# Hybrid encoder on one core: the order of loads and of the first norms ahead of the input product

## The chip, the cores and the metric

The kernel runs on one core of a Trainium2 chip. The metric is device microseconds for one execution of the whole program; the time before is the median of three runs. The engines are PE (TensorE, matrix products), DVE (VectorE), ACT (ScalarE), POOL (GpSimd) and SP (SyncE), which here only issues DMAs. Each runs its own instructions strictly in the order of the program and meets the others at semaphores.

## What is computed

One encoder layer over a sequence of 1024 tokens and one of 512, width 1024, all float32:

```python
h = rms_norm(x, g_mix) * (1.0 + scale1) + shift1      # shift, scale: silu(c) @ w_mod + b_mod, per sequence
z = h @ w_in                                           # 1024 -> 1536
u_f, u_r, u_g = split(z, 3)
y = concat([fourier_mixer(u_f), bidirectional_rglru(conv(u_r)) * gelu(u_g)])
x = x + gate1 * (y @ w_out)
h = rms_norm(x, g_mlp) * (1.0 + scale2) + shift2
x = x + gate2 * (square(relu(h @ w_ff1)) @ w_ff2)
y = rms_norm(x, g_final)
```

The change is in the first two lines: the norm, its scaling by the conditioning map, and the first two output tiles of `h @ w_in`.

## The kernel before

Activations are kept transposed, features on the 128 partitions, tokens along the free axis. The 1536 tokens are three chunks of 512: chunks 0 and 1 are the long sequence, chunk 2 the short one. The 1024 features are eight tiles k; two tiles make a quarter q. The input product runs over 12 output tiles; the first two (j = 0, 1) are done in the front for all three chunks while the norms are still being made. Each product of float32 accuracy is three matmuls (`three`, lines 779 to 781): low part of the weights, low part of the activations, high parts. So every operand is split into hi (ACT) and lo (DVE; the later weight tiles on POOL).

The front does the following; every step has a helper of its own.

- **Norm of chunk n.** ACT squares the eight tiles (`square`, L1192), DVE adds them up (`add_squares`, seven steps, L1817), PE sums over the partitions (`norm_sum`, L796), ACT takes the root (`root`, L1197), DVE the reciprocal (`rstd`, L1732), ACT makes four diagonal blocks of it (`diagonals`, L1204), PE spreads them to all partitions (`norm_spread`, L803), ACT copies the result out (`copy_rstd`, L1251).
- **Conditioning map, quarter q.** PE multiplies `silu(c)` with a 2 MiB block of `w_mod` (`mod_quarter`, L823), ACT copies the row (`mod_copy`, L1237), PE turns it into columns (`mod_quarter_sum`, L832), DVE adds the bias and makes the amplitude (`mod_quarter_columns`, L1774 and L1778).
- **Product of chunk c, quarter q.** DVE scales x (`front_scale`, L1797), ACT adds the shift and makes hi (`front_hi`, L1245), DVE makes lo (`front_lo`, L1806), PE does 12 matmuls (`front`).
- **Weight tiles 0 and 1.** ACT makes hi (`split_win_hi`, L1217), DVE lo (`split_win_lo`, L1785).

One mod row buffer and one bank serve all four quarters, so a quarter's product waits until ACT has copied the row before it. All loads go out on SP's queue in program order: vec, chunk 0 in two halves, chunk 1, quarter 0 of `w_mod`, weight tiles 0 and 1, quarter 1, chunk 2, quarters 2 and 3. A chunk and a quarter are 2 MiB each, a weight tile 512 KiB.

After the front PE goes on with output tiles 2 to 11, then come the recurrent and Fourier mixers, the output product and the MLP.

Of the kernel before, what the change touches and what calls it, by code (L numbers as in the profile page):

```python
# [36 lines left out]
P = 128  # L37
# [85 lines left out]
def build_encoder(nc, vec_d, xT_d, w_mod_d, w_mod1_d, w_in_d, w_gate_d, w_four_d, w_out_d, w_ff1_d, w_ff2_d,  # L123
# [3 lines left out]
    def sem(name):  # L127
        return ctx.enter_context(nc.semaphore(name))
# [240 lines left out]
    ld_x = [sem(f"ld_x{c}") for c in range(NCH)]  # L369
    ld_first = [[sem(f"ld_first{q}_{h}") for h in range(1 if q else 2)] for q in range(NQ)]  # L370
    ld_x0 = sem("ld_x0_rest")
    ld_sin = sem("ld_sin")
    ld_mod = [sem(f"ld_mod{i}") for i in range(2)]
    ld_wo = [sem(f"ld_wo{i}") for i in range(3)]
# [169 lines left out]
    def _(sp):  # L544
# [13 lines left out]
        def load_chunk(c):  # L558
            sp.dma_start(x[:, c, :, :], xT_d[:, c * CH:(c + 1) * CH].rearrange("(k p) n -> p k n", p=P)
                         ).then_inc(ld_x[c], 16)  # L560

        load_chunk(1)
        load_first(0)
        sp.dma_start(win_raw[:], w_in_d[TILES[0]]).then_inc(ld_win, 16)
        sp.dma_start(win_raw1[:], w_in_d[TILES[1]]).then_inc(ld_wg, 16)
        load_first(1)
        load_chunk(2)
        load_first(2)
        load_first(3)
        sp.dma_start(dft_head[:], dft_head_d).then_inc(ld_dft, 16)  # L570
        sp.wait_ge(win_lo_done, 1)
# [204 lines left out]
    def _(pe):  # L776
# [23 lines left out]
        def norm_spread(n):  # L800

            pe.wait_ge(rstd_done, n + 1)
            pe.matmul(norm_bank(n)[:], ones[:], norm_diag(n)[:], start=True, stop=True).then_inc(norm_bc, 1)  # L803
# [78 lines left out]
        pe.wait_ge(const_set, 4)  # L882
        norm_sum(0)
        pe.wait_ge(vec_dve, 2)
        norm_spread(0)
        mod_quarter(0)
        mod_quarter_sum(0)
        norm_sum(1)
        mod_quarter(1)
        norm_spread(1)  # L890
        front(0, 0)
        mod_quarter_sum(1)
        front(1, 0)
        mod_quarter(2)
        front(0, 1)
        mod_quarter_sum(2)
        front(1, 1)
        norm_sum(2)
# [273 lines left out]
    def _(act):  # L1172
        def square(n, k):

            c = chunk_of(n)
            if n < NN:
                act.wait_ge(ld_x0 if c == 0 and k >= FT else ld_x[c], 16)
            else:
                act.wait_ge(out_evac, (n - NN) * KD + k + 1)
            if shared(n):  # L1180
                if k == 0 and n == 2:
                    act.wait_ge(norm_mm, 1)
                dst = squares(n)[:, k, :]
            else:
                if n == NN and k == 0:
                    act.wait_ge(wo_lo_done, 16)
                elif k == 0:
                    act.wait_ge(norm_bc, n)
                elif k > 2:
                    act.wait_ge(sq_added, adds_v(n) + k - 2)  # L1190
                dst = n_acc[:] if k == 0 else n_sq[k % 2][:]
            act.activation(dst, x[:, c, k, :], ACT.Square).then_inc(sq_done, 1)  # L1192
# [55 lines left out]
        def copy_rstd(n):  # L1248

            act.wait_ge(norm_bc, n + 1)  # L1250
            act.activation(rstd_sb[n][:], norm_bank(n)[:], ACT.Copy).then_inc(rstd_copied, 1)  # L1251

        for k in range(KD):
            square(0, k)
        for k in range(2):
            square(1, k)
        root(0)
        square(1, 2)
        diagonals(0)
        for k in range(3, KD):  # L1260
            square(1, k)
        split_win_hi(0)
        split_win_hi(1)
        mod_copy(0)
        copy_rstd(0)
        root(1)
        front_hi(0, 0)
        diagonals(1)
        mod_copy(1)
        copy_rstd(1)  # L1270
# [436 lines left out]
    def _(dve):  # L1707
# [109 lines left out]
                dve.tensor_tensor(sq[:, a, :], sq[:, a, :], sq[:, b, :], ALU.add).then_inc(sq_added, 1)  # L1817

        add_squares(0)
        rstd(0)  # L1820
        add_squares(1)
        split_win_lo(0)
        split_win_lo(1)
        mod_quarter_columns(0)
        front_scale(0, 0)
        rstd(1)
        front_lo(0, 0)
        front_scale(1, 0)
        front_lo(1, 0)
        mod_quarter_columns(1)  # L1830
# [720 lines left out]
```

## Time and profile before

| | us |
|---|---|
| median of 3 runs (1422.76 to 1425.23) | 1424.35 |
| the profiled execution | 1427.07 |
| its span | 1425.3 |
| PE busy | 1392.2 |
| DVE busy | 807.9 |
| ACT busy | 592.1 |
| POOL busy | 472.8 |

The profile is that of one execution, 1.8 us of which lie around the span. Times in a timeline are counted from the start of the span. A row of the timeline merges neighbouring instructions of one line; the idle time before it and who ended it stand in brackets. PE's second pass over an operand of float32 gives a record of its own, so four products of `norm_sum` count x8.

### The profile page before, as it was taken

The numbers are of one execution on the slowest core, as the hardware profiler recorded it, in microseconds if no ns is written. First come the engines' busy times: TensorE is split into PE (matmuls) and PEld (weight loads), VectorE is DVE, ScalarE is ACT, GpSimd is POOL, SyncE is SP. The second block draws the span as 40 slices with busy tenths as digits, with TensorE's granted clock in tenths as the row PEclk, the third lists the DMA queues.
The fourth block names the chain that finished last, engine by engine and source line by source line (L and its number), as shares of the span: only waits on it lengthen the run. The fifth ranks groups of instructions, "written<-read, shape, count | busy, mean of one in ns | idle before, by whom it ended". The sixth has DMA issues, their size and how long they took to land.

```text
span 1425.3 us, 18554 instructions
## 1 busy us (share of the span) xinstructions
PE 1392.2 (98%) x7594; PEld 1183.4 (83%) x7594; DVE 807.9 (57%) x771; ACT 592.1 (42%) x719; POOL 472.8 (33%) x269
## 2 busy tenths in 40 slices
PE   4999999999999999999999999999999999999998
PEld 2776778898888788888888888888888888888887
DVE  4967688795438954454533454353656434344584
ACT  6667979665335632232222223232332222433241
POOL 0011102135003764565455454532232222233131
PEclk9999999999999999999999999999999999999998
DMA  9443421105310343343343334479997444445542
GB/s 369 161 154 141 133 96 38 45 23 189 143 60 30 111 159 115 121 149 121 139 154 115 126 118 161 158 266 388 377 390 289 148 148 148 162 175 198 203 177 89
DMA packets 75702, 231.31 MB, mean 162 GB/s; under 512 B 5729, under 2 KB 9953, under 8 KB 66786
## 3 DMA queue, kind: packets, MB, share of 16 engines
q1 hardware_dynamic: 75618, 230.12, 44.1%
q8 instruction: 61, 1.00, 0.3%
q14 instruction: 23, 0.19, 0.0%
HBM read 165.09 MB, written 65.01 MB: 161 GB/s over the span
## 4 chain that ended last, share of the span: by engine, by line
PE 53%; issue 2%; POOL 1%; ACT 0%; POOLq 0%
PE bank L785 18%; PE bank L786 18%; PE bank L787 18%; POOL x L2483 0%; ACT w_hi L1579 0%; POOL w_lo L2460 0%; POOL w_s L2436 0%; PE bank L1099 0%; POOL w_lo L2452 0%; PE bank L1092 0%; POOLq L2491 0%; POOL x L2489 0%; POOLq L2488 0%; POOLq L2450 0%
## 5 line engine op out<-in xcount | busy, mean ns | idle before, releaser
L785 PE MATMUL bank<-hin_hi,w_lo 128*128 128x512 f32 (+1 forms) x896 | 302.4, 338 | 0.0
L786 PE MATMUL bank<-hin_lo,w_hi 128*128 128x512 f32 (+1 forms) x896 | 302.0, 337 | 0.0
L787 PE MATMUL bank<-hin_hi,w_hi 128*128 128x512 f32 (+1 forms) x896 | 301.4, 336 | 0.0
L2218 DVE TENSOR_TENSOR hin_lo<-hin,hin_hi 128x3072 fp32r<-128x3072 f32 x28 | 138.9, 4963 | 201.8 <-ACT hin_hi L1591 201.8
L2460 POOL TENSOR_TENSOR w_lo<-w_raw,w_hi 128x2048 fp32r<-128x2048 f32 x28 | 129.6, 4628 | 327.6 <-ACT w_hi L1579 326.1
L785 PEld LDWEIGHTS bank<-hin_hi,w_lo 128*128 128x128 f32 x896 | 170.2, 190 | 18.4 <-issue 0.2
L786 PEld LDWEIGHTS bank<-hin_lo,w_hi 128*128 128x128 f32 x896 | 170.3, 190 | 17.8 <-issue 0.2
L787 PEld LDWEIGHTS bank<-hin_hi,w_hi 128*128 128x128 f32 x896 | 170.1, 190 | 17.8
L1579 ACT ACTIVATE w_hi<-w_raw 128x2048 fp32r<-128x2048 f32 x28 | 53.6, 1916 | 290.3 <-PE bank L787 184.6
L2452 POOL TENSOR_TENSOR w_lo<-w_raw,w_hi 128x512 fp32r<-128x512 f32 x51 | 73.8, 1447 | 200.1 <-ACT w_hi L1517 200.1
L1526 ACT ACTIVATE hid<-bank 128x768 f32<-128x768 f32 (+2 forms) x68 | 52.5, 772 | 163.3 <-PE bank L787 162.5
L785 PE MATMUL bank<-t_hi,w_lo 128*128 128x512 f32 (+1 forms) x320 | 111.8, 349 | 3.2 <-ACT hid L1526 1.5
L786 PE MATMUL bank<-t_lo,w_hi 128*128 128x512 f32 (+1 forms) x320 | 111.6, 349 | 0.0
L787 PE MATMUL bank<-t_hi,w_hi 128*128 128x512 f32 (+1 forms) x320 | 111.0, 347 | 0.0
L2452 POOL TENSOR_TENSOR w_lo<-w_s,w_hi 128x512 fp32r<-128x512 f32 x68 | 105.1, 1559 | 13.1 <-ACT w_hi L1517 9.8
L2386 POOL TENSOR_TENSOR win_lo<-win_raw,win_hi 128x1024 fp32r<-128x1024 f32 x10 | 26.9, 2694 | 221.3 <-ACT win_hi L1217 221.3
L2151 DVE TENSOR_TENSOR hid<-bank,hid 128x768 f32<-128x768 f32 (+2 forms) x17 | 15.5, 910 | 146.6 <-ACT hid L1526 146.6
L785 PE MATMUL bank<-hi_f,w_lo 128*128 128x512 f32 (+1 forms) x256 | 87.2, 341 | 2.7 <-POOL w_lo L2452 2.7
L786 PE MATMUL bank<-lo_f,w_hi 128*128 128x512 f32 (+1 forms) x256 | 87.1, 340 | 0.0
L787 PE MATMUL bank<-hi_f,w_hi 128*128 128x512 f32 (+1 forms) x256 | 86.8, 339 | 0.0
L785 PE MATMUL bank<-hi_r,w_lo 128*128 128x512 f32 (+1 forms) x256 | 86.7, 339 | 0.0
L786 PE MATMUL bank<-lo_r,w_hi 128*128 128x512 f32 (+1 forms) x256 | 86.5, 338 | 0.0
(293 smaller groups left out, 3110.8 us busy)
## 6 DMA issues: line engine op xcount, KB each, us to landing
hin<-hid_all SPq DMA_DIRECT2D x28, 1536.0 KB, 6.6
hid_all<-hid SPq DMA_DIRECT2D x105, 384.0 KB, 2.5
w_raw<-in_w_ff SPq DMA_DIRECT2D x36, 1024.0 KB, 8.9
w_raw<-in_w_ff SPq DMA_DIRECT2D x68, 256.0 KB, 2.9
mod_raw<-in_w_mod SPq DMA_DIRECT2D x16, 1024.0 KB, 5.3
x<-in_xT SPq DMA_DIRECT2D x5, 2048.0 KB, 13.4
w_sums<-w_raw SPq DMA_DIRECT2D x8, 1024.0 KB, 14.9
w_raw<-w_sums SPq DMA_DIRECT2D x8, 1024.0 KB, 10.3
```

The costliest lines, as they stand in the source:

```text
L785: pe.matmul(out, w_lo, v_hi, start=first, stop=False, skip_group_check=True)
L786: pe.matmul(out, w_hi, v_lo, start=False, stop=False, skip_group_check=True)
L787: return pe.matmul(out, w_hi, v_hi, start=False, stop=last, skip_group_check=True)
L1526: act.activation(hid[j][:, c0:c1], ps[:, buf + c0:buf + c1], ACT.Relu if i == P4 else ACT.Copy).then_inc(ff1_copy, 1)
L1579: act.activation(w2_hi[n % 2][:], w2_raw[m % RAWS][:], ACT.Copy).then_inc(w2_hi_done, 1)
L2151: m = dve.tensor_tensor(slot[S_T3][:, cols], out_of(1), slot[S_T3][:, cols], ALU.add)
L2218: dve.tensor_tensor(hin_lo[n % 3][:].rearrange("p t n -> p (t n)"), hin[n % 3][:].rearrange("p t n -> p (t n)"), hin_hi[n % 3][:].rearrang ...
L2386: pool.tensor_tensor(win_lo[win_of(j)][:].rearrange("p k m -> p (k m)"), raw[:], win_hi[win_of(j)][:].rearrange("p k m -> p (k m)"), ALU.s ...
L2452: pool.tensor_tensor(w1_lo[o % 4][:], src[:], w1_hi[o % 4][:], ALU.subtract).then_inc(w1_lo_done, 1)
L2460: pool.tensor_tensor(w2_lo[n % 2][:].rearrange("p t n -> p (t n)"), w2_raw[m % RAWS][:].rearrange("p t n -> p (t n)"), w2_hi[n % 2][:].rea ...
```

## The change

Four things are moved; no arithmetic is added or taken out.

1. SP: weight tiles 0 and 1 are loaded right behind chunk 0, then quarter 0, then chunk 1 in two halves with a semaphore each (a new one, `ld_x1`), quarters 1 and 2, chunk 2, quarter 3.
2. PE: `mod_quarter(0)` goes ahead of `norm_spread(0)`, `front(0, 0)` ahead of `norm_sum(1)`, and `mod_quarter(2)` behind `front(0, 1)`.
3. ACT: the two weight splits, `root(0)`, `diagonals(0)`, `mod_copy(0)` and `copy_rstd(0)` go ahead of chunk 1's squares, and `front_hi(0, 0)` behind two of those.
4. DVE: the two weight splits go ahead of `rstd(0)`, and the adds of chunk 1 behind `front_scale(0, 0)` (one) and `front_lo(0, 0)` (six).

```diff
     @block.sync
-        load_chunk(1)
-        load_first(0)
         sp.dma_start(win_raw[:], w_in_d[TILES[0]]).then_inc(ld_win, 16)
         sp.dma_start(win_raw1[:], w_in_d[TILES[1]]).then_inc(ld_wg, 16)
+        load_first(0)
+        for h, s in enumerate((ld_x[1], ld_x1)):
+            rows = xT_d[h * FT * P:(h + 1) * FT * P, CH:2 * CH]
+            sp.dma_start(x[:, 1, h * FT:(h + 1) * FT, :], rows.rearrange("(k p) n -> p k n", p=P)).then_inc(s, 16)
         load_first(1)
+        load_first(2)
         load_chunk(2)
-        load_first(2)
         load_first(3)
     @block.tensor
         norm_sum(0)
         pe.wait_ge(vec_dve, 2)
+        mod_quarter(0)
         norm_spread(0)
-        mod_quarter(0)
         mod_quarter_sum(0)
+        front(0, 0)
         norm_sum(1)
         mod_quarter(1)
         norm_spread(1)
-        front(0, 0)
         mod_quarter_sum(1)
         front(1, 0)
+        front(0, 1)
         mod_quarter(2)
-        front(0, 1)
         mod_quarter_sum(2)
         front(1, 1)
     @block.scalar
...
+                if c < 2 and k >= FT:
+                    act.wait_ge((ld_x0, ld_x1)[c], 16)
...
         for k in range(KD):
             square(0, k)
+        split_win_hi(0)
+        split_win_hi(1)
+        root(0)
+        diagonals(0)
+        mod_copy(0)
+        copy_rstd(0)
         for k in range(2):
             square(1, k)
-        root(0)
-        square(1, 2)
-        diagonals(0)
-        for k in range(3, KD):
+        front_hi(0, 0)
+        for k in range(2, KD):
             square(1, k)
-        split_win_hi(0)
-        split_win_hi(1)
-        mod_copy(0)
-        copy_rstd(0)
         root(1)
-        front_hi(0, 0)
         diagonals(1)
         mod_copy(1)
         copy_rstd(1)
     @block.vector
         add_squares(0)
-        rstd(0)
-        add_squares(1)
         split_win_lo(0)
         split_win_lo(1)
+        rstd(0)
         mod_quarter_columns(0)
         front_scale(0, 0)
+        add_squares(1, range(1))
+        front_lo(0, 0)
+        add_squares(1, range(1, KD - 1))
         rstd(1)
-        front_lo(0, 0)
         front_scale(1, 0)
```

PE at the start of the program, before. `sq_103` holds chunk 0's squares and `sq_other` chunk 1's, L803 is `norm_spread`, `mod_first_109` and `mod_first_110` are quarters 0 and 1:

```order
L803 MATMUL bank<-diag_first,ones 128x512 [waits rstd_done,vec_dve]
L823 MATMUL bank<-mod_first_109,c_silu 32x512 [waits ld_first0_0]
L823 MATMUL bank<-mod_first_109,c_silu 32x512 x3
L823 MATMUL bank<-mod_first_109,c_silu 32x512 [waits ld_first0_1]
L823 MATMUL bank<-mod_first_109,c_silu 32x512 x3
L832 MATMUL bank<-pick,mod_row 128x2 [waits mod_rows]
L832 MATMUL bank<-pick,mod_row 128x2 x3
L796 MATMUL bank<-ones,sq_other 128x1 [waits sq_added]
L796 MATMUL bank<-ones,sq_other 128x1 x3
L823 MATMUL bank<-mod_first_110,c_silu 32x512 [waits ld_first1_0,mod_rows]
L823 MATMUL bank<-mod_first_110,c_silu 32x512 x7
L803 MATMUL bank<-diag_first,ones 128x512 [waits rstd_done]
```

PE at the same place, changed (line numbers are 3 higher):

```order
L826 MATMUL bank<-mod_first_109,c_silu 32x512 [waits ld_first0_0,vec_dve]
L826 MATMUL bank<-mod_first_109,c_silu 32x512 x3
L826 MATMUL bank<-mod_first_109,c_silu 32x512 [waits ld_first0_1]
L826 MATMUL bank<-mod_first_109,c_silu 32x512 x3
L806 MATMUL bank<-diag_first,ones 128x512 [waits rstd_done]
L835 MATMUL bank<-pick,mod_row 128x2 [waits mod_rows]
L835 MATMUL bank<-pick,mod_row 128x2 x3
L782 MATMUL bank<-hi_f,win_lo_94 128x512 [waits hlo_done,win_lo_done]
L783 MATMUL bank<-lo_f,win_hi_92 128x512
...
L784 MATMUL bank<-hi_f,win_hi_93 128x512
L799 MATMUL bank<-ones,sq_other 128x1 [waits sq_added]
L799 MATMUL bank<-ones,sq_other 128x1 x3
```

Quarter 0 stands ahead of `norm_spread`, and the first products of `front(0, 0)` stand ahead of the sum over `sq_other`.

PE at quarter 2 of the map, before: the end of `front(1, 0)`, `mod_quarter(2)` (`mod_first_111`), the start of `front(0, 1)`:

```order
L780 MATMUL bank<-lo_f,win_hi_93 128x512
L781 MATMUL bank<-hi_f,win_hi_93 128x512
L823 MATMUL bank<-mod_first_111,c_silu 32x512 [waits ld_first2_0,mod_rows]
L823 MATMUL bank<-mod_first_111,c_silu 32x512 x7
L779 MATMUL bank<-hi_f,win_lo_94 128x512 [waits hlo_done]
L780 MATMUL bank<-lo_f,win_hi_92 128x512
```

PE there, changed: the end of `front(0, 1)`, then `mod_quarter(2)`, its sum and the start of `front(1, 1)`:

```order
L783 MATMUL bank<-lo_f,win_hi_93 128x512
L784 MATMUL bank<-hi_f,win_hi_93 128x512
L826 MATMUL bank<-mod_first_111,c_silu 32x512 [waits ld_first2_0,mod_rows]
L826 MATMUL bank<-mod_first_111,c_silu 32x512 x7
L835 MATMUL bank<-pick,mod_row 128x2 [waits mod_cols,mod_rows]
L835 MATMUL bank<-pick,mod_row 128x2 x3
L782 MATMUL bank<-hi_f,win_lo_94 128x512 [waits hlo_done]
```

`mod_quarter(2)` has moved behind the 12 products of `front(0, 1)`, and its sum follows it directly.

ACT in the same stretch, in the changed kernel: hi of chunk 1, quarter 0, then four squares of chunk 2, hi(0, 1), four squares, the copy of mod row 2, and the two tiles of hi(1, 1):

```order
L1251 ACTIVATE hi_f<-x,mod 128x512 [waits xn_done] x2
L1198 ACTIVATE sq_103<-x 128x512 [waits norm_mm,ld_x2]
L1198 ACTIVATE sq_103<-x 128x512 [waits ld_x2] x3
L1251 ACTIVATE hi_f<-x,mod 128x512 [waits xn_done] x2
L1198 ACTIVATE sq_103<-x 128x512 [waits ld_x2] x4
L1243 ACTIVATE mod_row<-bank 128x512 [waits mod_tr,mod_mm]
L1251 ACTIVATE hi_f<-x,mod 128x512 [waits xn_done] x2
```

Here nothing has moved: ACT has the same operations in the same order as before, with the copy of the row ahead of hi(1, 1).

## Rows read from the trace of the kernel before

**Rows 1.** The page: busy us, share of the span, instructions.

```profile
PE 1392.2 (98%) x7594; PEld 1183.4 (83%) x7594; DVE 807.9 (57%) x771; ACT 592.1 (42%) x719; POOL 472.8 (33%) x269
```

**Rows 2.** Table by stretch, the front and the rest: stretch, length, engines busy, clock, DMA.

```profile
0.00:77.00 77.00, 57.17 (x270) 38.00 (x270) 55.26 (x100) 47.42 (x84) 5.57 (x15) 0.96 0.64 245
77.00:1425.30 1348.30, 1334.98 (x7325) 1145.45 (x7324) 752.65 (x672) 544.66 (x636) 467.20 (x254) 1.00 0.43 158
```

**Rows 3.** Timeline, PE: start us, us, engine, line, operation, [idle before, who ended it].

```profile
14.03 1.84 PE L796 MATMUL bank<-ones,sq 128*128 128x1 f32 x8 [14.03 <-DVE sq L1817]
18.50 2.04 PE L803 MATMUL bank<-diag_first,ones 128*128 128x512 f32 x2 [2.63 <-ACT diag_first L1204]
20.47 3.61 PE L823 MATMUL bank<-mod_first,c_silu 128*32 128x512 f32 x16
...
28.15 3.64 PE L823 MATMUL bank<-mod_first,c_silu 128*32 128x512 f32 x16 [1.40 <-DMA mod_first<-in_w_mod]
...
32.81 1.42 PE L779 MATMUL bank<-hi_f,win_lo 128*128 128x512 f32 x1
...
37.44 0.49 PE L779 MATMUL bank<-hi_f,win_lo 128*128 128x512 f32 x1
...
40.39 1.92 PE L823 MATMUL bank<-mod_first,c_silu 128*32 128x512 f32 x16
42.25 0.50 PE L779 MATMUL bank<-hi_f,win_lo 128*128 128x512 f32 x1
...
49.33 1.05 PE L796 MATMUL bank<-ones,sq 128*128 128x1 f32 x8 [0.36 <-DVE sq L1817]
```

**Rows 4.** Timeline of the same front, ACT.

```profile
9.95 2.19 ACT L1192 ACTIVATE sq<-x 128x512 f32<-128x512 f32 x4 [0.53 <-DMA x<-in_xT]
...
36.55 2.18 ACT L1192 ACTIVATE sq<-x 128x512 f32<-128x512 f32 x4
...
42.38 0.60 ACT L1237 ACTIVATE mod_row<-bank 128x512 f32<-128x512 f32 x1
42.88 1.33 ACT L1245 ACTIVATE hi_f<-x,mod 128x512 fp32r<-128x512 f32 x2
```

**Rows 5.** Timeline of the same front, DVE.

```profile
18.91 4.08 DVE L1817 TENSOR_TENSOR sq_other<-sq_other 128x512 f32<-128x512 f32 x6 [1.45 <-ACT sq_other L1192]
...
34.47 1.41 DVE L1797 SCALAR_TENSOR_TENSOR x<-x,amp,rstd_sb 128x512 f32<-128x512 f32 x2 [4.99 <-ACT rstd_sb L1251]
36.01 1.41 DVE L1806 SCALAR_TENSOR_TENSOR lo_f<-x,mod,hi_f 128x512 fp32r<-128x512 f32 x2
...
44.28 1.41 DVE L1806 SCALAR_TENSOR_TENSOR lo_f<-x,mod,hi_f 128x512 fp32r<-128x512 f32 x2
46.13 0.23 DVE L1774 TENSOR_TENSOR mod<-bank,vec 128x4 f32<-128x4 f32 x2 [0.44 <-PE bank L832]
```

**Rows 6.** Table by stretch, from lo(1, 1) to the last lo of the front.

```profile
44.28:73.04 28.76, 27.72 (x138) 21.15 (x137) 26.29 (x49) 15.21 (x26) 0.71 (x1) 1.00 0.21 77
```

**Rows 7.** Timeline, SP: the issues of the second win tile, quarter 1, chunk 2.

```profile
8.77 1.47 SPq L565 DMA_DIRECT2D win_raw<-in_w_in  x1
10.29 1.32 SPq L553 DMA_DIRECT2D mod_first<-in_w_mod  x2
11.65 0.81 SPq L559 DMA_DIRECT2D x<-in_xT  x1
```

**Rows 8.** DMA issues, those three loads: KB, us from issue to landing.

```profile
win_raw<-in_w_in SPq DMA_DIRECT2D x1, 512.0 KB, 14.2
...
mod_first<-in_w_mod SPq DMA_DIRECT2D x1, 1024.0 KB, 17.1
...
x<-in_xT SPq DMA_DIRECT2D x1, 2048.0 KB, 21.8
```

**Rows 9.** Table by stretch, where the granted clock (PEclk) changes.

```profile
27.30:27.40 0.10, 0.00 (x0) 0.00 (x0) 0.10 (x1) 0.10 (x1) 0.00 (x0) 0.61 1.00 369
34.10:34.20 0.10, 0.10 (x2) 0.10 (x1) 0.00 (x0) 0.10 (x1) 0.00 (x0) 0.75 1.58 655
```

More of the change, by code:

```diff
@@ L371, in build_encoder @@
     ld_x0 = sem("ld_x0_rest")
+    ld_x1 = sem("ld_x1_rest")
     ld_sin = sem("ld_sin")
@@ L1176, in square @@
             if n < NN:
-                act.wait_ge(ld_x0 if c == 0 and k >= FT else ld_x[c], 16)
+                if c < 2 and k >= FT:
+                    act.wait_ge((ld_x0, ld_x1)[c], 16)
+                else:
+                    act.wait_ge(ld_x[c], 16)
             else:
```

## The prediction

> **What bounds the kernel now.** I read the page first: PE is busy 1392.2 us of the span, 98% [rows 1]. The table by stage gives the place: in the first 77.00 us PE is busy for 57.17, in the other 1348.30 for 1334.98 [rows 2]. So the front is where PE can gain or lose much, and PE's later waits are ended by other engines, which all move when PE's front moves. The third view is the timeline of the front, engine by engine [rows 3 to 5], where the reader is to see when each step starts and who released it. Chunk 0 of the input product starts at 32.81, chunk 1 at 37.44, chunk 0's second quarter at 42.25. From there on PE has nearly no gap, but DVE is nearly as full: from 44.28 (lo of chunk 1, quarter 1) to 73.04 it is busy 26.29 of 28.76 [rows 6]. DVE runs in order and makes each lo just ahead of the product that needs it, so a late lo there shifts the rest of the front.
>
> Below, front(c, q), hi(c, q), lo(c, q), scale(c, q) are the product, its ACT operand, its DVE operand and DVE's scaling for chunk c and quarter q; mq(q) is mod_quarter, sum(q) is mod_quarter_sum.
>
> **The loads.** Landings go in issue order: the second win tile lands at 8.77 + 14.2 = 22.97, mod_first of quarter 1 at 10.97 + 17.1 = 28.07, chunk 2 at 11.65 + 21.8 = 33.45 [rows 7, 8] (10.97 is the second of the two issues that begin at 10.29). That is 2 MiB in 5.1 to 5.4 us. The second half of chunk 0 is there at 9.95 [rows 4]. Ahead of quarter 0 there stand now only 1 MiB of win tiles, so quarter 0 lands at 9.95 + 2.6 + 5.1 = 17.6. Chunk 1 follows at about 22.9, before ACT needs it. Quarter 1 stays at 28.1. Chunk 2 has one 2 MiB load more ahead of it: 33.45 + 5.1 = 38.55.
>
> The Trainium skill, "DMA: Bandwidth & Descriptors" (Queues, rings and completion order), says that descriptors of a ring are consumed in order but that a later one may finish its write before an earlier one. By the first half chunk 2 lands at 38.55, by the second it could be a little earlier; the three landings above agree with the first half.
>
> **Front of chunk 0.** norm_sum(0) still ends at 14.03 + 1.84 = 15.87. mq(0) now follows at once: half of it, then the half that waits for 17.6, 1.8 us at the low clock (3.61 whole [rows 3]), so it ends at 19.5. norm_spread(0) 2.04: 21.5. sum(0) 1.0 to 1.8 (the 1.84 of norm_sum(0) is an equal set of small products at the low clock): 22.9. Columns 0.6 (four small DVE steps, 0.23 a pair [rows 5]), scale 0.75, hi 0.7, one add of squares, lo 0.75: front(0, 0) starts at about 26.4 instead of 32.81. The two win splits on ACT and DVE fill time in which both stood idle. This is what the change wins on paper: 6.4 us for 12 products.
>
> **Norm of chunk 1.** It is now behind that. DVE's six remaining adds start after lo(0, 0), at 26.9, and take 4.08 [rows 5]: 31.0, where before they ended at 22.99. norm_sum(1) waits for them and for front(0, 0), which at the low clock takes 2.95 x 1.88 = 5.5 (2.95 is front(1, 0), 37.44 to 40.39; 1.88 is 3.61 over 1.92, mq at either clock): 31.9. Between 31.0 and 31.9 it starts. It takes 1.0. From its end to norm_spread, over root, reciprocal and diagonals, chunk 0 took 15.87 to 18.50, 2.6, with a square of 0.6 in between on ACT: 2.0. norm_spread 1.0, half of 2.04: 35.0 to 35.9. mq(1) (1.92, its data there since 28.1) lies under the root and the diagonals. Row copy 0.6, then 2.3 for scale, hi and lo of the first tile (34.47 to 36.01 + 0.75 [rows 5]): front(1, 0) starts at 37.9 to 38.8, take 38.2. Before it started at 37.44 [rows 3]. So the 6.4 us won by front(0, 0) end as an idle PE, and front(1, 0) is 0.8 later; that alone would cost 0.8.
>
> **Quarter 1.** Here is the loss. Before, PE did mq(2) at 40.39, ahead of front(0, 1), so ACT could take the mod row at 42.38 and make hi(1, 1) at 42.88 [rows 3, 4]. Now mq(2) stands behind front(0, 1), while ACT's order still has the copy of mod row 2 ahead of hi(1, 1). Queued behind that copy on ACT are all hi of chunk 1's quarter 1 and of quarter 2; DVE waits for them at lo(1, 1), and behind that wait stand the last four adds of chunk 2's squares and everything later. The chain:
> chunk 2 lands 38.55; four squares, 2.18, which stand on ACT ahead of hi(0, 1): 40.75; hi 0.7 (1.33 for two): 41.5; lo 0.75: 42.25; front(0, 1) starts at 42.3, as before, but with mq(2) not done. front(0, 1) 2.95, as front(1, 0): 45.2. mq(2) 1.9: 47.1. Row copy, next ACT start 0.5 later (42.38 to 42.88): 47.6. hi 0.7: lo(1, 1) starts at 48.4 against 44.28: **+4.1**. Off goes DVE's 0.44 wait for sum(2) at 46.13, which now comes earlier than its turn: **+3.7**. The rest of the front keeps its order and lengths, and DVE has little slack in it, so the front's end moves by this.
> If chunk 2 landed early, ACT would still end hi(1, 0) at about 38.2 and the squares at 40.4: 0.4 to 0.6 less, +3.1. That is the lower bound of this term.
>
> **The clock.** The granted clock goes from 1.00 to 0.50 (1.2 GHz) at 27.35, 3.3 us after mq(0) ended at 24.07, with only 1- and 2-column products between; it is back at 1.00 (2.4 GHz) at 34.15, 6.0 us after mq(1) began at 28.15 [rows 9]. The column reads 1.00 also in the first 24 us, but mq(0) took 3.61 there against 1.92 for mq(2): low. A gap of 0.36 + 1.05 us around norm_sum(2) [rows 3] did not lower it. In the changed kernel PE has, from the end of norm_spread(1) to front(1, 0), 0.6 + 2.3 + 0.1 = 3.0 us with only sum(1) in it. That is far nearer to 3.3 than to 1.4, so I take it that the clock falls there. Price: front(1, 0) 5.5 instead of 2.95, from 38.2 to 43.7, so front(0, 1) starts 1.4 later than 42.3; back high 6.0 after 38.2, at 44.2, so 0.5 us more at half rate, 0.25. Together **+1.6**. Ends: 0 if it stays; if all of front(0, 1) is at the low clock too, 1.4 + 2.9 x 0.88 = 3.9.
>
> The Trainium skill, "TensorE: Matmul & The Clock Gate" (HAM oscillation — how this bites in real kernels), says that waits between bursts of matmuls let the clock fall, so that the next burst starts slow. By that rule the sum is +5.3, without it +3.7; the fall at 27.35 agrees with it.
>
> **Sum.** 3.7 + 1.6 = +5.3 us. The profiled execution took 1427.07 (span 1425.3), the median of the runs is 1424.35; a shift of the front adds the same to either. 1424.35 + 5.3 = **1429.6**. A difference under 0.2% (2.85 us) is about what a measurement of this kernel can't tell from none.
>
> **Rivals.**
> 1. The clock stays high in the 3.0 us gap. For: 3.0 is shorter than 3.3. Against: the nearer row. +3.1 to +3.7: 1427.5 to 1428.1.
> 2. The clock is low for longer, through front(0, 1). For: in the front of before it was slow to return twice, and the new gap before mod row 2 (copy and sum, about 0.8) may add to it. +3.7 + 3.9 = +7.6: 1432.0.
> 3. Not slower: DVE makes the loss up behind lo(1, 1). While ACT waits for mq(2), DVE has done scale(1, 1) and the first adds, and its stretch from there holds 28.76 - 26.29 = 2.5 of waits, 0.44 of them already counted. It would decide if those waits vanished: 3.7 less 2.0 is +1.7, 1426.1, no measurable change. Against: each is the latency of a chain (root, reciprocal, diagonals, spread, copy) that starts from DVE's own late adds, so it comes along.
> 4. Faster: the products of front(0, 0), some 3 us of PE, count in full because PE is the bound. They are off the dense stretch only if front(1, 0) comes before about 34.5; the adds alone end at 31.0 and the norm chain to it is 7 us. 1424.35 less 3: 1421.3.
>
> **How the numbers follow.** Forecast 0.42, rival 1 0.28, rival 2 0.18, rival 3 0.09, rival 4 0.03. Slower by over 0.2%: 0.42 + 0.28 + 0.18, less 0.03 for the edge of rival 1 near 1427.2: 0.85. Within: 0.12. Faster: 0.03. The range leaves out rivals 3 and 4 and the tail of rival 2: 1427.0 (+2.65, just under rival 1) to 1432.8 (+8.4, rival 2 with 0.8 more at the low clock).
>
> **What would show each step.** Quarter 0's products run by 19.5 and front(0, 0) starts near 26.4; DVE ends chunk 1's adds near 31; front(1, 0) starts near 38.2; ACT's squares of chunk 2 begin near 38.5 and after a DMA wait; ACT waits about 4 us for mq(2) before mod row 2, and DVE waits 3 to 6 us at lo(1, 1), which starts at 48.4 to 50; the clock column shows 0.5 around 38 to 44. DVE's last lo, which ended at 73.04, ends at 76.5 to 81. Wrong would be: lo(1, 1) before 47, a last lo before 75.5, or a later stage whose PE waits shrink by as much as the front grew.

## Result: the change costs 3.8 us

The changed kernel takes 1428.18 us (median of 9 runs, 1427.59 to 1430.29) against 1424.35 for the kernel before (9 runs, 1422.15 to 1425.23), a ratio of 1.0033 with a 95% interval of 1.0024 to 1.0041. The prediction was 1429.6, range 1427.0 to 1432.8. The profiled execution of the changed kernel has a span of 1426.3, only 1.0 over that of before, while the medians are 3.8 apart. The section on the 2.5 us below shows where that difference comes from.

Page and table by stretch, changed kernel (against [rows 1, 2]; columns as there):

```profile
PE 1391.6 (98%) x7594; PEld 1183.8 (83%) x7594; DVE 813.4 (57%) x771; ACT 591.9 (41%) x719; POOL 472.9 (33%) x269
...
0.00:77.00 77.00, 54.44 (x255) 37.30 (x256) 51.57 (x96) 46.07 (x82) 2.39 (x14) 0.93 0.64 245
77.00:1426.30 1349.30, 1337.14 (x7341) 1146.46 (x7339) 761.78 (x676) 545.79 (x638) 470.54 (x256) 1.00 0.43 157
```

In the first 77 us PE has done 2.7 us less work (54.44 against 57.17), and the mean clock of the stretch is 0.93 instead of 0.96. The loss is in the front, as expected, but the two 77 us windows end at different points of the program. The front's end is better marked by the first product over `mod_raw`: 80.66, and 77.09 before. That is **+3.57**. (A second profile of each kernel gave 75.63 and 80.27, so this figure is good to about 1.5 us; see e8 and e10.)

Timeline of PE, changed kernel (against [rows 3]; line numbers on PE are 3 higher; the last row is that end mark):

```profile
15.26 3.36 PE L826 MATMUL bank<-mod_first,c_silu 128*32 128x512 f32 x16
18.55 1.13 PE L806 MATMUL bank<-diag_first,ones 128*128 128x512 f32 x2
...
23.94 0.47 PE L782 MATMUL bank<-hi_f,win_lo 128*128 128x512 f32 x1 [3.48 <-DVE lo_f L1811]
...
28.49 1.05 PE L799 MATMUL bank<-ones,sq_other 128*128 128x1 f32 x8
...
31.42 1.12 PE L806 MATMUL bank<-diag_first,ones 128*128 128x512 f32 x2
...
35.65 0.77 PE L782 MATMUL bank<-hi_f,win_lo 128*128 128x512 f32 x1 [2.32 <-DVE lo_f L1811]
...
41.51 0.50 PE L782 MATMUL bank<-hi_f,win_lo 128*128 128x512 f32 x1 [1.53 <-DVE lo_f L1811]
...
44.49 1.92 PE L826 MATMUL bank<-mod_first,c_silu 128*32 128x512 f32 x16
47.13 1.05 PE L835 MATMUL bank<-pick,mod_row 128*128 128x2 f32 x8 [0.72 <-ACT mod_row L1243]
48.53 0.62 PE L782 MATMUL bank<-hi_f,win_lo 128*128 128x512 f32 x1 [0.34 <-DVE lo_f L1811]
...
52.97 0.95 PE L799 MATMUL bank<-ones,sq 128*128 128x1 f32 x8
...
80.66 1.07 PE L814 MATMUL bank<-mod_raw,c_silu 128*32 128x512 f32 x8
```

(L799 is `norm_sum`, L826 `mod_quarter`, L806 `norm_spread`, L835 `mod_quarter_sum`; L782 is the first product of a front.) Front(0, 0) starts at 23.94 instead of 32.81, nearly 9 us earlier, and it buys nothing lasting: PE stands idle 3.48 before it and 2.32 before front(1, 0), which comes at 35.65, 1.8 earlier than 37.44. Front(0, 1) at 41.51 is still 0.7 earlier than before. Then mq(2), now behind it, starts at 44.49 instead of 40.39. Sum(2), and with it the whole of quarter 1 of chunk 1, hangs on that.

ACT and DVE, changed kernel (against [rows 4, 5]; ACT lines are 6 higher, DVE lines 5):

```profile
37.87 2.19 ACT L1198 ACTIVATE sq<-x 128x512 f32<-128x512 f32 x4 [2.48 <-DMA x<-in_xT]
...
46.49 0.60 ACT L1243 ACTIVATE mod_row<-bank 128x512 f32<-128x512 f32 x1 [3.12 <-PE bank L826]
46.98 1.32 ACT L1251 ACTIVATE hi_f<-x,mod 128x512 fp32r<-128x512 f32 x2
...
24.37 4.06 DVE L1822 TENSOR_TENSOR sq_other<-sq_other 128x512 f32<-128x512 f32 x6
...
33.21 1.41 DVE L1802 SCALAR_TENSOR_TENSOR x<-x,amp,rstd_sb 128x512 f32<-128x512 f32 x2 [3.16 <-ACT rstd_sb L1257]
...
40.70 1.41 DVE L1811 SCALAR_TENSOR_TENSOR lo_f<-x,mod,hi_f 128x512 fp32r<-128x512 f32 x2 [2.68 <-ACT hi_f L1251]
...
47.73 1.42 DVE L1811 SCALAR_TENSOR_TENSOR lo_f<-x,mod,hi_f 128x512 fp32r<-128x512 f32 x2 [2.35 <-ACT hi_f L1251]
49.06 0.22 DVE L1779 TENSOR_TENSOR mod<-bank,vec 128x4 f32<-128x4 f32 x2
...
60.28 2.74 DVE L1802 SCALAR_TENSOR_TENSOR x<-x,amp,rstd_sb 128x512 f32<-128x512 f32 x4 [1.25 <-ACT rstd_sb L1257]
...
73.94 2.73 DVE L1811 SCALAR_TENSOR_TENSOR lo_r<-x,mod,hi_r 128x512 fp32r<-128x512 f32 x4
```

ACT reaches the copy of mod row 2 and waits 3.12 us for PE (the product of mq(2)); hi(1, 1) is queued behind it. DVE waits 2.35 at lo(1, 1), which starts at 47.73 instead of 44.28: +3.45. From there the sum closes by rows. The wait of 0.44 at the columns [rows 5] is gone (49.06 has none); the columns start 1.33 after lo(1, 1), where they started 1.85 after it before, 0.52 less. DVE's wait for `rstd_sb` at 60.28 is 1.25, where the same wait before was 0.62. 3.45 - 0.52 + 0.63 = 3.56. The row of the last lo starts at 73.94, which is 3.55 after the same row before:

```profile
56.72 2.74 DVE L1797 SCALAR_TENSOR_TENSOR x<-x,amp,rstd_sb 128x512 f32<-128x512 f32 x4 [0.62 <-ACT rstd_sb L1251]
...
70.39 2.73 DVE L1806 SCALAR_TENSOR_TENSOR lo_r<-x,mod,hi_r 128x512 fp32r<-128x512 f32 x4
```

From lo(1, 1) to that row it takes 26.21 us, and 26.11 before. DVE won nothing back on this stretch.

Table by stretch, changed kernel, inside the three stretches at the low clock (24.8 to 28.2, 35.1 to 38.5, 48.7 to 52.1; against [rows 9]):

```profile
24.90:25.00 0.10, 0.10 (x1) 0.00 (x1) 0.10 (x1) 0.10 (x1) 0.00 (x0) 0.50 1.37 573
...
35.20:35.30 0.10, 0.00 (x0) 0.00 (x0) 0.10 (x1) 0.10 (x1) 0.00 (x0) 0.50 1.17 430
...
48.80:48.90 0.10, 0.10 (x1) 0.05 (x1) 0.10 (x1) 0.00 (x0) 0.00 (x0) 0.50 0.00 0
52.00:52.10 0.10, 0.10 (x2) 0.10 (x1) 0.10 (x1) 0.00 (x0) 0.00 (x0) 0.50 0.00 0
```

Each of the three begins within 1.2 us after a product start that had waited, or in the wait itself. Front(0, 0) takes 4.55 (23.94 to 28.49), front(1, 0) runs at half rate to 38.5, front(1, 1) takes 4.44 (48.53 to 52.97). The first costs nothing: norm_sum(1), next on PE, has to wait for DVE's adds anyway, and these end at 24.37 + 4.06 = 28.43.

### The profile page after: what moved, and what is told of

It is laid out like the page before. It is cut to its first block, busy times and chain, and to the rows that moved or that the text cites. A ratio compares the mean times of both kernels' runs of the same rounds, so it can differ in the third digit from the quotient of the medians.

```text
span 1426.3 us, 18555 instructions
## 1 busy us (share of the span) xinstructions
PE 1391.6 (98%) x7594; PEld 1183.8 (83%) x7594; DVE 813.4 (57%) x771; ACT 591.9 (41%) x719; POOL 472.9 (33%) x269
## 4 chain that ended last, share of the span: by engine, by line
PE 53%; issue 2%; POOL 1%; ACT 0%; POOLq 0%
PE bank L788 18%; PE bank L789 18%; PE bank L790 18%; POOL x L2489 0%; ACT w_hi L1584 0%; POOL w_lo L2466 0%; POOL w_s L2442 0%; PE bank L1102 0%; POOL w_lo L2458 0%; PE bank L1095 0%; POOLq L2497 0%; POOL x L2495 0%; POOLq L2494 0%; POOLq L2456 0%
## 5 line engine op out<-in xcount | busy, mean ns | idle before, releaser
L1522 ACT ACTIVATE w_hi<-w_s 128x512 fp32r<-128x512 f32 x68 | 42.8, 631 | 106.4 <-POOL w_s L2448 44.7
```

What stands on the lines that cost most here:

```text
L1522: act.activation(w1_hi[o % 4][:], src[:], ACT.Copy).then_inc(w1_hi_done, 1)
```

## Experiments

The theory (A): two steps cost the time, mq(2) behind front(0, 1) and the later load of chunk 2, plus the clock. Its rivals are B, that the loss is the later load alone, and C, that it is the low clock in the front. "Front end" is the start of the first product over `mod_raw` in the profiled execution: 77.09 before, 80.66 changed. Timed results are medians of the runs, with the ratio to the kernel before on the same chip (the medians of that kernel were 1423.42 for e1 to e4, 1423.63 for e5 to e8, 1423.82 for e9 to e12). The ratio is worked out from all the runs and can differ a little from that of the medians.

| | median us | ratio, 95% | front end | clock at 1.2 GHz, 20 to 60 us |
|---|---|---|---|---|
| changed | 1428.18 | 1.0033 [1.0024, 1.0041] | 80.66 | 24.8-28.2, 35.1-38.5, 48.7-52.1 |
| e10, changed again | 1427.92 | 1.0025 [1.0015, 1.0035] | 80.27 | 23.5-30.3, 37.2-40.6 |
| e8, before again | 1424.13 | 1.0003 [0.9994, 1.0011] | 75.63 | 25.0-31.8 |
| e1, mq(2) back | 1425.53 | 1.0017 [1.0008, 1.0026] | 77.69 | 22.2-29.0, 35.8-39.2 |
| e2, chunk 2 back | 1427.65 | 1.0030 [1.0021, 1.0039] | 78.22 | 24.9-28.3, 35.2-38.6 |
| e3, both back | 1426.70 | 1.0019 [1.0010, 1.0028] | 78.61 | 23.7-30.5, 37.3-40.7 |
| e4, row copy late | 1427.22 | 1.0025 [1.0016, 1.0034] | 79.28 | 24.9-28.3, 35.1-38.6 |
| e5, before, mq(2) behind | 1425.45 | 1.0009 [1.0001, 1.0018] | 79.03 | 26.5-33.3, 47.0-50.4 |
| e6, before, PE kept busy | 1422.46 | 0.9990 [0.9982, 0.9999] | 74.72 | none |
| e12, e6 again | 1422.21 | 0.9992 [0.9983, 1.0001] | 74.70 | none |
| e7, changed, PE kept busy | 1429.36 | 1.0047 [1.0033, 1.0061] | 84.01 | 42.0-48.8 |
| e11, e7 and one gap more | 1431.06 | 1.0047 [1.0033, 1.0061] | 82.57 | 31.5-34.9 |
| e9, e3, PE kept busy | 1425.05 | 1.0012 [1.0003, 1.0021] | 77.65 | 30.1-33.6 |

### mod_quarter(2) put back

```diff
         front(1, 0)
-        front(0, 1)
         mod_quarter(2)
+        front(0, 1)
```

> The changed kernel with one step undone: mod_quarter(2) stands ahead of front(0, 1) again, the rest as changed. Theory A (the copy of mod row 2 stands on ACT ahead of hi(1, 1) and now waits for the late mod_quarter(2)): mod_quarter(2) runs while PE otherwise idles before 41.5, ACT has the row by its turn at 43.4, lo(1, 1) starts at 45.3 instead of 47.73 and the front ends 2.4 us earlier: about 1425.8. Theory B (the loss is chunk 2's load standing one 2 MiB block later): nothing changes before lo(0, 1) at 40.7, less than 0.7 us gained: 1427.5 to 1428.2. Theory C (the loss is the low clock in the front): the third low stretch vanishes because the gap around the mod row goes, 0.6 us at most.

Measured: 1425.53, where 1425.8 was expected. Against the before on its own chip it is +2.1, the changed kernel +3.8 and +4.1: this one step is worth about 2 of the 4 (the intervals of the two ratios, 1.0008 to 1.0026 and 1.0024 to 1.0041, just touch). In the trace ACT's copy of row 2 no longer waits, and lo(1, 1) follows:

```profile
43.37 0.58 ACT L1243 ACTIVATE mod_row<-bank 128x512 f32<-128x512 f32 x1
...
40.80 1.42 DVE L1811 SCALAR_TENSOR_TENSOR lo_f<-x,mod,hi_f 128x512 fp32r<-128x512 f32 x2 [2.01 <-ACT hi_f L1251]
...
45.39 1.41 DVE L1811 SCALAR_TENSOR_TENSOR lo_f<-x,mod,hi_f 128x512 fp32r<-128x512 f32 x2
```

The row is copied at 43.37 (46.49 in the changed kernel) and lo(1, 1) starts at 45.39, 2.34 earlier. It is still 1.1 later than before; there chunk 2's squares are the late end (they start at 37.97, after a DMA wait of 1.82).

### Chunk 2 ahead of quarter 2, and both put back

```diff
         load_first(1)
-        load_first(2)
         load_chunk(2)
+        load_first(2)
```

E2 has this edit alone, e3 this edit and that of e1.

> The changed kernel with chunk 2 loaded ahead of quarter 2 of the map, as before; PE's order stays changed. Theory A: the chain over mod_quarter(2) stays and only starts sooner: ACT's squares of chunk 2 start near 35.4 instead of 37.87, front(0, 1) starts when front(1, 0) ends at 39.8 instead of 41.5, lo(1, 1) starts at 45.8 instead of 47.7: 1.9 us gained, about 1426.3, still 2 us over the kernel before. Theory B: all the loss goes, 1424.4. Theory C: no change worth measuring.

> The changed kernel with both undone: mod_quarter(2) ahead of front(0, 1) and chunk 2 loaded ahead of quarter 2. What is left of the change is the early front of chunk 0 (weights, quarter 0, front(0, 0) ahead of chunk 1's norm). Theories A and B together: lo(1, 1) at 43.0, the sum over mod row 2 at 44.6 is what DVE waits for next, the last adds of chunk 2 end at 48.7 against 52.2 in the changed kernel and 49.3 before: 3.4 us under the changed kernel, about 1424.8, the same as the kernel before. If the early front of chunk 0 itself cost something, it stays above 1426; if it gained its paper value, it falls under 1422.

The trace of e2 does what the theory says. ACT's squares of chunk 2 start at 35.37 without a wait (37.87 after a DMA wait of 2.48 in the changed kernel), and lo(1, 1) at 45.95, 1.78 earlier. The front ends at 78.22, 2.4 earlier. But the timed runs do not follow: 1427.65 with runs from 1425.35 to 1430.92, against 1426.3 expected. The profiled execution was the fastest of its eleven, and the one with the highest mean clock: 0.996, where nine of the other ten had 0.992 to 0.994 and one 0.995. So it is not a typical one. The load order costs about 1.8 at lo(1, 1) in the traces; in the timed runs no cost of it is shown, neither between e2 and the changed kernel (1.0021 to 1.0039 against 1.0024 to 1.0041) nor between e3 and e1 (1.0010 to 1.0028 against 1.0008 to 1.0026). Rival B is out all the same: with the load order put back the loss stays.

E3 was a miss: 1424.8 expected, 1426.70 measured. What is left of the change when both steps are undone still costs a ratio of 1.0010 to 1.0028, over half of the whole loss (3.3 of some 4 us by the medians, 1.0019 of 1.0033 by the ratios). So the two steps of theory A are not the whole account, and the costs of the parts don't add up: taking one bound away uncovers the next, and this next one is the early front of chunk 0. The chain of waits is seen in DVE's rows:

```profile
35.04 1.41 DVE L1802 SCALAR_TENSOR_TENSOR x<-x,amp,rstd_sb 128x512 f32<-128x512 f32 x2 [3.16 <-ACT rstd_sb L1257]
...
45.17 1.41 DVE L1811 SCALAR_TENSOR_TENSOR lo_f<-x,mod,hi_f 128x512 fp32r<-128x512 f32 x2 [0.52 <-ACT hi_f L1251]
```

Scale(1, 0) comes at 35.04 (34.47 before, 33.23 in e8), lo(1, 1) at 45.17 (44.28 before, 42.82 in e8). The norm of chunk 1 now stands behind front(0, 0). PE idles for 3.48 ahead of front(0, 0), which then runs at 1.2 GHz from 25.05 to 30.30, while DVE's adds for chunk 1 were ready at 29.55. The early front itself gains nothing and costs, by the interval, 1.4 to 4.0 us. (E1 alone came out lower than e3, with overlapping intervals; the order of these two is not settled.)

### ACT's copy of row 2 behind hi(1, 1)

```diff
             square(2, k)
-        mod_copy(2)
         front_hi(1, 1)
+        mod_copy(2)
         front_hi(0, 2)
```

> The changed kernel with one ACT step moved: the copy of mod row 2 behind hi(1, 1) instead of ahead of it; PE's and SP's orders stay changed. Theory A says that what hurts is the copy blocking hi(1, 1): hi(1, 1) then follows the squares at 43.4, lo(1, 1) starts when DVE's adds are done, 45.3 instead of 47.7. The mod row is still late, so DVE next waits for its columns until about 48.1 and the last adds end 1 us earlier than in the changed kernel: about 1427.2. If lo(1, 1) does not move, theory A has the wrong place.

Measured 1427.22, as expected, though its interval (1.0016 to 1.0034) doesn't part it from the changed kernel; the rows do. It tests the place of the loss: PE keeps the changed order, only ACT's queue differs.

```profile
46.56 0.60 ACT L1243 ACTIVATE mod_row<-bank 128x512 f32<-128x512 f32 x1 [1.89 <-PE bank L826]
...
45.37 1.41 DVE L1811 SCALAR_TENSOR_TENSOR lo_f<-x,mod,hi_f 128x512 fp32r<-128x512 f32 x2
48.30 0.23 DVE L1779 TENSOR_TENSOR mod<-bank,vec 128x4 f32<-128x4 f32 x2 [1.53 <-PE bank L835]
```

Lo(1, 1) moves from 47.73 to 45.37: what held it was the copy queued ahead of it, not PE. But the late row then holds the columns of quarter 2 (1.53 of wait at 48.30), so the front ends only 1.4 earlier. Moving the copy frees hi(1, 1), but doesn't make mq(2) any earlier.

### The step alone, in the kernel before

```diff
         front(1, 0)
-        mod_quarter(2)
         front(0, 1)
+        mod_quarter(2)
```

> The kernel before with one part of the change alone: mod_quarter(2) behind front(0, 1). Theory A (that row's copy then stands late on ACT ahead of hi(1, 1)): front(0, 1) starts when lo(0, 1) is there, 40.5 instead of 42.25, ends at 43.4, the map product at 45.3, lo(1, 1) at 46.6 instead of 44.28: the front ends 1.8 to 2.3 us later and the time is about 2 us over the kernel before. Theory C (only the clock matters): within 0.7 us of the kernel before.

Measured 1425.45: +1.8 on the same chip's 1423.63, where +2 was expected (the ratio is 1.0009, 0.1 to 2.6 us by its interval). ACT waits again at the row:

```profile
44.88 0.60 ACT L1237 ACTIVATE mod_row<-bank 128x512 f32<-128x512 f32 x1 [3.07 <-PE bank L823]
...
46.12 1.42 DVE L1806 SCALAR_TENSOR_TENSOR lo_f<-x,mod,hi_f 128x512 fp32r<-128x512 f32 x2 [2.35 <-ACT hi_f L1245]
```

Waits of 3.07 and 2.35 are those of the changed kernel (3.12 and 2.35). Taken out of the changed kernel or put into the one before, the step is worth about 2 us. It is what bounds the front of the changed kernel. That it is the largest part of the loss is not shown: without it and without the moved load, e3 still loses 1.4 to 4.0.

### What the clock costs

The extra products are `ones` times `ones`, 128 columns into a free bank; nobody reads them. E6, e7, e9, e11 and e12 carry them as added work. In the kernel before:

```diff
         mod_quarter(0)
+        keep_busy(2)
         mod_quarter_sum(0)
         norm_sum(1)
+        keep_busy(5)
         mod_quarter(1)
```

> The kernel before with seven extra products of 128 columns of ones, written to a bank that nobody reads until it is started anew: two after mod_quarter(0) and five after norm_sum(1), where PE waits. They keep PE busy over the gap before mod_quarter(1), so that it should stay at 2.4 GHz there. Theory C (low clock in the front costs time): mod_quarter(1) takes 1.92 instead of 3.64 and norm_spread(1) 1.0 instead of 2.08, chunk 1's scaling starts 2.8 us sooner, and with quarter 2's landing at 38.4 as the next bound the front ends about 2 us sooner: 2 us under the kernel before. If the clock falls all the same, or if the front is bound elsewhere: no gain, or 0.5 us lost to the extra products.

> e6_before_pe_busy once more, unchanged, since its gain is near what the rounds can tell: if the high clock over mod_quarter(1) is what it gains, again 0.999 times the kernel before within 0.0009, no stretch at 1.2 GHz after 22, and the first product of mod_raw near 74.7.

Both runs of it hold in kind: 1422.46 and 1422.21, -1.2 and -1.6 on the chip's own before, where e6 expected -2; front end 74.72 and 74.70. It is the fastest version of this study, though only just beyond what can be told from no change (0.9992, interval to 1.0001, the second time). The clock shows no fall from 20 to 60 us, and mq(1) takes 1.92 instead of 3.64:

```profile
27.64 1.92 PE L823 MATMUL bank<-mod_first,c_silu 128*32 128x512 f32 x16 [0.35 <-DMA mod_first<-in_w_mod]
...
38.03 1.93 PE L823 MATMUL bank<-mod_first,c_silu 128*32 128x512 f32 x16 [0.98 <-DMA mod_first<-in_w_mod]
```

mq(2) now waits 0.98 for its load: the next limit behind the clock is the DMA. So before's low stretch costs 0.9 to 2.4 us at the front's end (75.63 or 77.09 less 74.7). In this kernel the slow products stand ahead of chunk 1's norm, so the clock has a price. If it were also the reason of the change's loss (rival C), the changed kernel would lose less with its gaps filled. That comes next.

Kept before again, for the scatter of a baseline:

> The kernel before, unchanged, profiled and timed once more: what its front does in another execution. Its profiled execution took 2.7 us more than its median. If that came from the front, this one shows a shorter stretch at 1.2 GHz and a front that ends 1 to 2 us before 77.09; if it came from the later stages, the front ends at 77.1 again and PE's later waits are fewer. The ratio to the kernel before shows what five rounds can tell: 1.0000 within 0.0009.

The same program gave a front end of 75.63 where the first profile had 77.09. The low stretch lay at 25.0 to 31.8 instead of 27.3 to 34.1, so the chain to scale(1, 0) was through at 33.23 instead of 34.47. A profile of one execution fixes the front no better than 1.5 us.

In the changed kernel I tried the same in each gap. This is e11; e7 lacks the 12 ahead of front(0, 1):

```diff
         mod_quarter_sum(0)
+        keep_busy(13)
         front(0, 0)
...
         mod_quarter_sum(1)
+        keep_busy(9)
         front(1, 0)
+        keep_busy(12)
         front(0, 1)
         mod_quarter(2)
+        keep_busy(3)
         mod_quarter_sum(2)
+        keep_busy(1)
```

> The changed kernel with extra products of the same kind in its gaps: 13 ahead of front(0, 0), 9 ahead of front(1, 0), 4 around the sum over mod row 2. Theory A: all three products that ran at 1.2 GHz take 2.95 again, but only the third had a consumer waiting for it (norm_sum(2) came 0.75 after its adds), so 0.6 us are gained: about 1427.6. Theory C: the low clock is the loss, and 2 to 4 us come back: 1424.3 to 1426.

> e7_after_pe_busy with 12 more of the extra products in the gap that was left, between front(1, 0) and front(0, 1). There e7 idled 4.1 us and then ran front(0, 1) and mod_quarter(2) at 1.2 GHz, ahead of mod row 2 and hi(1, 1). If that is why e7 was slower than the changed kernel: front(0, 1) takes 2.95 and mod_quarter(2) 1.92, lo(1, 1) starts at 47 to 48 instead of 51.7, and the time is 0 to 0.7 us under the changed kernel, 1427 to 1428. If the extra products themselves slow the loads or the kernel: it stays near 1429.4.

Both were misses: 1429.36 and 1431.06, above the changed kernel's 1427.92 and 1428.18, where equal or less was expected. (By the intervals, 1.0033 to 1.0061 for both against 1.0024 to 1.0041, it is shown only that they are not clearly faster. The profiled execution of e7, at 1434.48, was the slowest of its six, four of which took 1429.14 to 1429.39, so its waits may be longer than the usual ones.) In e7 the first gaps no longer lower the clock; the next one, unfilled, does, and there it costs:

```profile
42.74 0.80 PE L782 MATMUL bank<-hi_f,win_lo 128*128 128x512 f32 x1 [4.07 <-DVE lo_f L1820]
...
39.10 2.19 ACT L1207 ACTIVATE sq<-x 128x512 f32<-128x512 f32 x4 [3.69 <-DMA x<-in_xT]
...
50.48 0.60 ACT L1252 ACTIVATE mod_row<-bank 128x512 f32<-128x512 f32 x1 [5.89 <-PE bank L826]
```

PE idles 4.07 before front(0, 1) and is then at 1.2 GHz from 42.0 to 48.8, which covers front(0, 1) and mq(2), the two pieces ACT is waiting for: ACT's wait at row 2 grows from 3.12 to 5.89. In e11 that gap is filled, but a fixed count of products cannot know how long the gap is. Front(0, 1) started at 44.14, though its lo, begun at 41.94, was ready near 42.7; and a low stretch came earlier, over mq(1).

In both, chunk 2 was also there for ACT only at 39.10, where the others with this order had 37.87 to 38.10. The DMA views show what came in between. The load of chunk 2 itself is issued at the same time and takes longer (e7, then e11, the window around its issue):

```profile
x<-in_xT SPq DMA_DIRECT2D x1, 2048.0 KB, 23.4
```

```profile
x<-in_xT SPq DMA_DIRECT2D x1, 2048.0 KB, 23.5
```

It is 22.2 in the changed kernel. Between 32 and 36 us, where chunk 2 is the load that is next or coming in, both have one packet on another DMA queue, whose kind the profile calls instruction (e7):

```profile
q8 instruction: 1, 0.02, 1.7%
```

In the changed kernel there is none from 32 to 36; the same line stands in its window from 40 to 44, when chunk 2 has landed. This packet, 16 KB and 1.0 to 1.2 us long, is in all fourteen profiled executions (both kernels and e1 to e12), and in each of them the load that is coming in or next lands some 0.8 to 1.5 us late: chunk 2 in e7 and e11 (packet at 32.1 and 34.0), a half of quarter 2 in e9 (35.9), half of quarter 3 in all the others (37.7 to 42.0). The five executions with added products have it before 38, the nine others after 39.9. So part of what e7 and e11 lost is a side effect of the added instructions: their packet comes earlier, and in these two it hits the load on which front(0, 1) waits. That is in part the second case of e11's expectation, in which the extra products slow the loads. No run was made to test it; it rests on the order of these rows. It also means that the changed kernel was never seen with a high clock throughout and chunk 2 on time. That rival C is no more than the smaller part rests on the rows (0.6 us at front(1, 1)) and on e1 and e5, not on these two runs.

> The changed kernel with mod_quarter(2) and chunk 2's load put back (as in e3_both_back) and with extra products that nobody reads in the two gaps of PE ahead of front(0, 0) and front(1, 0). It tells what of the 2.7 us that e3_both_back still lost is the clock. Its profile had 1.2 GHz from 23.7 to 30.5 and from 37.3 to 40.7, and chunk 1's scaling at 35.0. If that is the clock: scaling of chunk 1 at 33.3, lo(1, 1) near 43, front end near 76.5 (78.6 there), time about 1.7 us less, 1425.0. If the early front of chunk 0 costs by its order alone: stays at 2.7 us over the kernel before.

E9 is e3 with the first two fills. It met its number (1425.05, 1425.0 expected), but not by the means that it assumed: the clock fell at 30.1, over mq(1), after a wait of 1.56 before norm_sum(1). Even with both moved steps undone and two gaps filled, the early front does not come below the kernel before (1.0012, 1.0003 to 1.0021). Since the clock fell here too, this doesn't tell what the early front costs by its order alone.

> The changed kernel, unchanged, beside the others on one chip. All theories: 1.0033 times the kernel before, within 0.001. Its profile shows how the stretches at 1.2 GHz lie in another execution: the first product of mod_raw (80.66 in the first profile) between 79 and 82, chunk 2's squares again after a DMA wait near 38, and 3 us of waiting on ACT before mod row 2.

The changed kernel again gave 1427.92, front end 80.27. Its low stretches lay elsewhere (none over front(1, 1)), but lo(1, 1) started at 47.97 and the end moved by 0.4 only. In these two executions the place of the fall hardly matters; in e7, where it falls on front(0, 1) and mq(2), it does.

### Where 2.5 us went in the profiled executions

The front's end is 3.57 later, but the span only 1.0 longer. The rest of the span, from the front's end on, was 1348.2 in before's profile and 1345.6 in the changed one's. Over all executions it lies in two groups: 1347.5 to 1348.7 (before, e5, e7, e8, e9) and 1345.1 to 1346.3 (changed, e1, e2, e3, e4, e6, e10, e11, e12). Tables by stretch of 10 us, before and then e1:

```profile
500.00:510.00 10.00, 7.67 (x39) 6.43 (x39) 9.19 (x10) 4.44 (x7) 7.68 (x3) 0.93 0.50 160
510.00:520.00 10.00, 10.00 (x52) 8.66 (x51) 4.38 (x5) 2.36 (x4) 7.65 (x6) 0.90 0.35 129
```

```profile
500.00:510.00 10.00, 7.67 (x45) 6.59 (x45) 9.79 (x11) 4.38 (x6) 7.07 (x3) 1.00 0.45 148
510.00:520.00 10.00, 10.00 (x61) 8.90 (x60) 5.37 (x5) 2.71 (x4) 7.77 (x6) 1.00 0.40 143
```

And the same gap of PE in either, before and then e1:

```profile
507.20 0.50 PE L785 MATMUL bank<-hi_f,w_lo 128*128 128x512 f32 x1 [2.33 <-POOL w_lo L2452]
```

```profile
507.81 0.50 PE L788 MATMUL bank<-hi_f,w_lo 128*128 128x512 f32 x1 [2.33 <-POOL w_lo L2458]
```

PE waits 2.33 for POOL's `w_lo` in both, for the same product. In before the clock is then at 0.50 for some 3.4 us (508.6 to 512), in e1 it stays at 1.00. All five executions of the longer kind, and none of the nine others, have such a stretch, between 506 and 530. It lies 430 us behind the change and comes with both orders: with that of before in before, e5 and e8, not in e6 and e12; with the changed one in e7 and e9, not in the seven others. All five were also above the median of their kernel, by 0.9 to 5.1 us; the nine others were at it or below it. So the timed runs seem to be mostly of the shorter kind. The mean clock recorded with each run fits that: 0.993 and 0.994 in the two profiled executions of before, 0.995 to 0.997 in 81 of the 86 runs of it that were timed beside the experiments. The long kind would account for before's profile, at 1427.07, standing 2.7 over its median, and for the two spans showing 1.0 where the medians show 3.8. The medians agree with the front (+3.57, or +3.2 to +5.0 over the two profiles of each kernel).

## Why the prediction held, and where its steps were off

- **Where the kernel is bound.** Right. All that the change moved is visible in the front, and front +3.57 fits median +3.8. That the two are so close is in part luck of the pair of profiles: with the second profile of before the front is 5.0 later.
- **The loads.** Chunk 2: 38.55 predicted, 37.87 by ACT's row. Right. The rule from the Trainium skill, "DMA: Bandwidth & Descriptors" (Queues, rings and completion order), that a later descriptor may finish its write before an earlier one, was not needed: the landing came where issue order puts it, 0.7 early. Quarter 0 was there sooner than 17.6: mq(0) ran from 15.26 for 3.36 without a wait, and norm_spread(0) at 18.55 took 1.13, the clock already high.
- **Front of chunk 0.** Right in kind, too late by 2.5 (26.4 against 23.94): 0.5 from an earlier start, the rest from quarter 0 and from small steps priced at the low clock.
- **Norm of chunk 1.** The chain is the one that was named (adds behind lo(0, 0), then sum, root, spread). It was forecast 2.5 too late as well (38.2 against 35.65), so front(1, 0) was 1.8 earlier than before, not 0.8 later. The statement that the early front ends as idle PE held (3.48 and 2.32). But it was priced at 0.8 by itself, and e3, where the two steps of quarter 1 are undone, measures 1.4 to 4.0. The forecast did not need this term, since in the changed kernel chunk 2 and mq(2) come later still. It matters once these two are put back, and there e3's expectation missed it.
- **Quarter 1.** The bound of the changed kernel is where the prediction put it. ACT's wait is 3.12 (about 4 forecast), lo(1, 1) +3.45 (+4.1), the 0.44 of DVE is gone. The term of +3.7 measured +2.9 here; it was too high mainly since chunk 2 landed 0.7 earlier than worked out. The rows of e1, e4 and e5 show the mechanism. Two of the signs fell outside their limits: lo(1, 1) at 47.73 (48.4 to 50 forecast) and DVE's wait there, 2.35 (3 to 6).
- **The clock.** The mis-sized term. One fall was forecast, from 38 to 44, with 1.6 of cost. There were three, each 3.4 long. The one over front(1, 0) came (35.1 to 38.5) and cost nothing, since front(0, 1) waited until 41.51 for lo. The price is about 0.6, at front(1, 1): norm_sum(2) at 52.97 came 0.75 after DVE's adds ended (49.46 + 2.74 = 52.2), and DVE's wait for `rstd_sb` grew by 0.63. The Trainium skill, "TensorE: Matmul & The Clock Gate" (HAM oscillation — how this bites in real kernels), says that waits between bursts of matmuls let the clock fall, so that the next burst starts slow. The trace agrees for three gaps (3.48, 2.32, and 0.72 with 0.34) and not for a fourth (1.53, before front(0, 1)). By that rule alone all three would be added to the time, and by the rows only one was.
- **Sum.** 3.7 + 1.6 = 5.3 predicted; 2.9 + 0.6 = 3.5 by the rows. The measured number lies between rival 1 (1427.5 to 1428.1, clock stays high) and the forecast, next to rival 1. It is near it in size only: the clock did fall, off the critical path.
- **Rivals 3 and 4.** DVE did not make the loss up: 26.21 us from lo(1, 1) to the row of the last lo, 26.11 before. And front(1, 0) at 35.65 was close to the 34.5 from which rival 4 would have paid, but lo(1, 1) hangs on chunk 2 and mq(2), not on front(1, 0).

Open: why e2's timed runs were mostly at a lower mean clock than its profile and keep so little of the 2.4 us that the trace gained, how the 3.8 us divide between the order of mq(2) and the early front, and what decides whether the stretch near 508 comes.

## What to carry to other kernels

When a producer is moved back on one engine, look through the queues of its consumers for the copy that waits for it, and for what stands behind that copy: ACT's 0.60 us row copy held a chain that had no need of it. An operand made early is worth only what the next late input allows; here the first front came 9 us sooner and the next late input (chunk 2, mq(2)) moved back. Price a fall of the clock at the consumer that waits, not by the products it slows, and do not trust a span difference of 1 to 3 us between two single profiles. When one step is undone and the loss doesn't go with it, look for the next bound before the theory is given up or kept: here two chains were late, and each alone cost some 2 to 3 us (e5, e3). And products added to fill a gap are instructions too: they bring the DMA packets of the instruction queue forward, onto other loads.

## What the runs showed of the chip

- Every low stretch in the front lasted 3.4 or 6.8 us, in the twelve executions that had one; the prediction had taken 6.0 from the start of the next burst. Its place moved by 1.3 to 2.3 us between two executions of one program (24.8 and 23.5 in the changed kernel, 27.3 and 25.0 before).
- The same gap of 2.33 us was followed by a low stretch in before, and by none in e1.
- Filling some gaps moved the low stretch to the next unfilled one (e7, e9, e11); in the kernel before (e6, e12) filling took it away. Seven products of 128 columns were worth 1.2 to 1.6 us of 1424, measured twice (0.9990 and 0.9992, the second interval up to 1.0001).
- Mq(0) took 3.36 us (3.61 before) and mq(2) 1.92, while the clock column read 1.00 over both.
- In all fourteen profiled executions one 16 KB packet of the queue of kind instruction came between 32 and 42 us, took 1.0 to 1.2 us, and the load coming in or next landed 0.8 to 1.5 us late. In e7 and e11 that was chunk 2: 23.4 and 23.5 us from issue to landing, 22.2 in the changed kernel.
